# Moving the memory's key and value projection from between the attention steps to between the gathered slots

## What is computed

```python
# first block
h = rms_norm(x); proj = h @ w_in                      # six groups of 512 columns
mq, mk, dq, dk = rope(rms_norm_per_head(...))         # groups 0 to 3; groups 4, 5 are values
x = x + concat(attention_8_heads, differential_attention_4_heads) @ w_out
h = rms_norm(x)
q = h @ peer_query                                    # 8 heads x 2 halves of 128
scores = q . sub_keys                                 # top 16 of each half, top 16 of their 256 sums
# per token and head: 16 experts, so 128 per token
act = gelu(expert_down[e] . h) * gate
x = x + sum_e act * expert_up[e]
# second block
... x = x + mixer(x) @ w_o
k, v = split(rms_norm(mem) @ w_xkv)                   # depends on mem alone
x = x + attention(h @ w_xq, k, v) @ w_xo
x = x + squared_relu_mlp(rms_norm(x)); return rms_norm(x)
```

## Time and profile before

| what | before |
|---|---|
| median of 3 runs | 1484.51 us (1483.87 to 1485.71) |
| the profiled execution's own time | 1484.1 us |
| its span, first to last instruction | 1482.3 us |
| PE, DVE, ACT, POOL busy | 85%, 54%, 41%, 61% |
| bytes moved | 400.70 MB, 268.45 MB of them by the gathers |
| first gather issued, last dot product | 260.0 us, 932.3 us |

### The profile page before, as it was taken

How to read it: one execution, slowest core, us unless ns; L and a number is a source line. 1 busy time by engine, 2 the same in 40 slices (tenths; PEclk the granted TensorE clock), 3 DMA queues, 4 the chain that set the end, 5 groups by cost and what they waited for, 6 DMA issues and landing times.

```text
span 1482.3 us, 17608 instructions
## 1 busy us (share of the span) xinstructions
PE 1264.4 (85%) x5876; PEld 897.6 (61%) x5876; DVE 802.3 (54%) x1512; ACT 600.5 (41%) x1255; POOL 909.5 (61%) x541
## 2 busy tenths in 40 slices
PE   7878888868778877777787787899999989999997
PEld 6667768723333333333333332589999968799886
DVE  5953334287776666677777754251255353259501
ACT  5455544343222333233233222345655435555432
POOL 7973476764444435544444452297878766599985
PEclk9999898979999889889888999899999999999999
DMA  7433345899999999999999999155553744456662
GB/s 250 141 128 107 121 128 179 336 384 420 420 420 420 420 420 420 420 420 421 420 417 418 395 421 406 71 184 186 157 171 117 227 139 144 128 161 196 193 191 99
DMA packets 72944, 400.70 MB, mean 270 GB/s; under 512 B 8096, under 2 KB 8352, under 8 KB 39712
## 3 DMA queue, kind: packets, MB, share of 16 engines
q0 software_dynamic: 36864, 268.45, 43.8%
q1 hardware_dynamic: 33696, 123.35, 26.2%
q10 hardware_dynamic: 2304, 7.85, 1.5%
HBM read 396.48 MB, written 3.15 MB: 270 GB/s over the span
## 4 chain that ended last, share of the span: by engine, by line
PE 29%; issue 22%; POOL 18%; DMA 18%; DVE 11%; ACT 2%; POOLq 0%; ACTq 0%; SPq 0%; DVEq 0%
POOL w_lo L1133 15%; DMA arena<-in_experts,arena 15%; PE bank L689 8%; PE bank L507 6%; PE bank L508 6%; PE bank L509 6%; DMA late_rows<-in_experts,arena 2%; DVE arena L1378 1%; DVE arena L1382 1%; DVE arena L1380 1%; POOL stat L1107 1%; POOL arena L1172 1%; DVE arena L1432 1%; DVE arena L1381 1%; ACT arena L988 1%
## 5 line engine op out<-in xcount | busy, mean ns | idle before, releaser
L1133 POOL TENSOR_TENSOR w_lo<-ring,w_hi 128x1024 fp32r<-128x1024 f32 x228 | 579.1, 2564 | 182.6 <-ACT w_hi L839 182.1
L689 PE MATMUL bank<-arena,diag 128*128 128x512 f32 x872 | 431.6, 653 | 120.4 <-ACT diag L994 120.3
L1172 POOL DMA_INDIRECT arena<-in_experts,arena x218 | 247.5, 1135 | 277.1 <-PE bank L689 225.4
L689 PEld LDWEIGHTS bank<-arena,diag 128*128 128x128 f32 x872 | 180.0, 210 | 369.5 <-issue 226.6
L1432 DVE CUSTOM_DVE_ANT_0 arena<-arena 128x1024 f32<-128x1024 f32 x218 | 262.1, 1225 | 157.7 <-DMA arena<-in_experts,arena 157.5
L839 ACT ACTIVATE w_hi<-ring 128x1024 fp32r<-128x1024 f32 x228 | 240.6, 1059 | 228.0 <-PE bank L509 188.4
L507 PE MATMUL bank<-hT_hi,w_hi 128*128 128x256 f32 x864 | 249.6, 289 | 18.1 <-POOL w_lo L1133 8.2
L508 PE MATMUL bank<-hT_lo,w_hi 128*128 128x256 f32 x864 | 247.3, 286 | 0.0
L509 PE MATMUL bank<-hT_hi,w_lo 128*128 128x256 f32 x864 | 247.1, 286 | 0.0
L985 ACT ACTIVATE arena<-arena 128x4 f32<-128x4 f32 x64 | 13.1, 205 | 439.0 <-DVE arena L1432 439.0
L507 PEld LDWEIGHTS bank<-hT_hi,w_hi 128*128 128x128 f32 x864 | 168.9, 195 | 19.6 <-issue 11.7
(11 more groups left out here) (214 smaller groups left out, 1559.0 us busy)
## 6 DMA issues: line engine op xcount, KB each, us to landing
ring<-in_stream SPq DMA_DIRECT2D x228, 512.0 KB, 3.5
arena<-in_experts,arena POOLq DMA_INDIRECT x218, 18.5
kv_park<-arena ACTq DMA_DIRECT2D x8, 256.0 KB, 3.8
arena<-kv_park ACTq DMA_DIRECT2D x1, 2048.0 KB, 9.1
x_res<-in_x SPq DMA_DIRECT2D x2, 512.0 KB, 5.4
arena<-in_mem SPq DMA_DIRECT2D x1, 1024.0 KB, 11.4
arena<-in_sub_keys ACTq DMA_DIRECT2D x1, 1024.0 KB, 6.3
out<-arena SPq DMA_DIRECT2D x2, 512.0 KB, 2.6
```

The source lines that it names most:

```text
L689: mm = pe.matmul(y_banks[half][:, :], diag[:, slot % DIAGS, :], rows_buf[slot % GATHERS][:, D + 512 * half:D + 512 * half + 512], start=(i ...
L1133: nc.gpsimd.tensor_tensor(w_lo[:, slot, :], ring[:, slot, :], w_hi[:, slot, :].bitcast(F32), ALU.subtract).then_inc(S("lo_made"), 1)
L1172: nc.gpsimd.indirect_dma_start(out=rows_buf[b], out_offset=None, in_=experts, in_offset=bass.IndirectOffsetOnAxis(ap=expert_u[:, slot:slot ...
```

## The change

- The stream's order is `w_in`, `w_out`, `query`, `xk`, `xv`, and the rest as before. PE does `xk` and `xv` ahead of slots 32, 48, 64, 80 (two chunks each), 112 and 152 (four each). ACT copies their results twelve slots later into one of two stages and writes them to DRAM, and makes the high parts there. POOL makes low parts ahead of gathers 60 and 76 (two each), 104, 140 and 184 (four each; the last four are of `in_nat`).
- Eleven buffers up to slot 186, 13 after that, since `hT` must stay until `xv` is done. A second split form `first_hT` serves `w_out` and `query`. `queryT` has two places in place of eight. The dot product writes its elementwise result over the row that it read.
- `sub_keys` and `ffn_rows` are asked for ahead of the norm, with no wait for the writes to DRAM.
- The rotation reads its operand from PSUM, and ACT no longer copies groups 0 to 3. DVE makes the low parts of chunks 3 and 5. The low parts of `w_in` are all made ahead of the memory's norm.
- The last four slots are weighed as 2, 1 and 1.

```diff
+MEMORY_AT = {32: ("xk", 0), 48: ("xk", 1), 64: ("xk", 2), 80: ("xk", 3), 112: ("xv", 0), 152: ("xv", 1)}
+MEMORY_OUT = {slot + 12: piece for slot, piece in MEMORY_AT.items()}
+LOW_AT = {60: 6, 76: 8, 104: 12, 140: 16, 184: 20}
+LAST_BATCHES = [(SLOTS - 4, 2), (SLOTS - 2, 1), (SLOTS - 1, 1)]
+BUFFER = [s % 11 if s < 187 else (s - 176) % GATHERS for s in range(SLOTS)]
-STREAM = [("w_in", 24), ("xk", 8), ("xv", 8), ("w_out", 8), ("query", 16),
+STREAM = [("w_in", 24), ("w_out", 8), ("query", 16), ("xk", 8), ("xv", 8),
...
+DVE_CHUNKS = [FIRST["w_in"] + 3, FIRST["w_in"] + 5]
...
@@ PE, attention steps
             for step in range(16):
-                memory(step)
...
@@ PE, slots
+                    if slot in MEMORY_AT:
+                        memory(*MEMORY_AT[slot])
                     pe.wait_ge(S("diag_made"), slot + 1)
...
@@ ACT, w_in
-                    copy_out(("w_in", n, t), proj1[n][:, t, :])
+                    else:
+                        copy_out(("w_in", n, t), proj1[n][:, t, :])
...
@@ ACT, ahead of the ffn norm
+            act.dma_start(subk, sub_keys).then_inc(S("subk_loaded"), 16)
+            act.dma_start(gain_rows, ffn_rows).then_inc(S("gain_loaded"), 16)
             sumsq("ffn", xs, xn, (0,))
             norm_out("ffn", con("g_ffn"))
             sumsq("ffn", xs, xn, (1,))
-            act.wait_ge(S("kv_parked"), 16 * 8)
-            act.dma_start(subk, sub_keys).then_inc(S("subk_loaded"), 16)
-            act.dma_start(gain_rows, ffn_rows).then_inc(S("gain_loaded"), 16)
...
@@ ACT, slots
+                    if slot in MEMORY_OUT:
+                        name, n = MEMORY_OUT[slot]
+                        park(memory_keys(name, n), name, n)
+                        hi_parts(memory_keys(name, n)[0][1] + RING)
+                    if slot < SLOTS - BATCH:
+                        weigh(slot)
+                    else:
+                        for i, count in LAST_BATCHES:
+                            weigh(i, count)
...
@@ POOL
+                    elif made[0] in DVE_CHUNKS:
+                        pool.wait_ge(S("lo_by_dve"), DVE_CHUNKS.index(made[0]) + 1)
+                        nc.gpsimd.memset(lo_mark[:, i:i + 1], 0.0).then_inc(S("lo_made"), 1)
...
+            lo_parts(LAST["w_in"])
             norm("mem")
-            lo_parts(LAST["xv"])
+            lo_parts(FIRST["w_out"] + RING - 1)
...
+                if slot in LOW_AT:
+                    lo_parts(FIRST["xk"] + LOW_AT[slot] - 1)
...
@@ DVE, rotation
+            low_part(DVE_CHUNKS[0])
...
+            low_part(DVE_CHUNKS[1])
             for g in range(4):
...
-                    qt = pg[:, t * 512:(t + 1) * 512].rearrange("p (h m n) -> p h m n", m=w, n=64)
+                    bank = take(dve, ("w_in", g, t))
+                    qt = bank[:, :].rearrange("p (h m n) -> p h m n", m=w, n=64)
...
@@ DVE, dot
-                if slot >= 2:
-                    dve.wait_ge(S("dots"), slot - 1)
-                v.tensor_tensor_reduce(out=dot_junk[slot % 2], ...
+                v.tensor_tensor_reduce(out=rows_buf[b][:, 0:D], ...
```

More of the change, by code:

```diff
@@ L134, in plan @@
     for step in range(12 + 4):
-        for keys, _, _ in memory_work(step):
-            for key, chunk in keys:
-                add(key, chunk)
         if step < 12:
@@ L144, in plan @@
             add(("pv", step - 4))
-    for keys, _, _ in memory_work(16):
-        for key, chunk in keys:
-            add(key, chunk)
     for g in range(4):
@@ L156, in plan @@
             add(("sub", h - 1))
-    for t in range(TT):
-        for half in range(2):
-            add(("y", t, half))
+    for slot in range(SLOTS):
+        if slot in MEMORY_AT:
+            for key, chunk in memory_keys(*MEMORY_AT[slot]):
+                add(key, chunk)
+        if slot % (SLOTS // TT) == 0:
+            for half in range(2):
+                add(("y", slot // (SLOTS // TT), half))
     norm("mix")
@@ L222, in maps_of, with memory_keys @@
     return [unit] if unit < 8 else [8 + 2 * (unit - 8), 9 + 2 * (unit - 8)]
[L226 to L233 removed]
+def memory_keys(name, n):
+    if name == "xk":
+        return [((name, n), FIRST[name] + 2 * n + 1)]
+    return [((name, n, t), FIRST[name] + 4 * n + 3) for t in range(TT)]
 def split_order():
@@ L315, in build @@
         minus_half = stats(24)
+        lo_mark = stats(2)
         hT = [(hT_hi[:, k, :], hT_lo[:, k, :]) for k in range(KT)]
+        hT_1 = [(first_hT[:, 0, k, :], first_hT[:, 1, k, :]) for k in range(KT)]
+        hT_of = {m: hT_1 if m == "ffn" else hT for m in NORMS}
         xn = tiles(A(0, 2048))
@@ L331, in build @@
         mem, memn = tiles(A(22784, 2048)), tiles(A(24832, 2048))
-        stage = [A(8192 + 512 * i, 512) for i in range(6)] + [A(29440 + 512 * i, 512) for i in range(2)]
+        stage = [A(7168 + 512 * i, 512) for i in range(2)]
         hd_ss = [stats(16) for _ in range(4)]
@@ L628, in _, with memory @@
                 wait_evacuated(pe, ("w_in", 5, t))
-            def memory(step):
-                for _, name, n in memory_work(step):
-                    if name == "xk":
-                        transposed(name, n)
-                    else:
-                        natural(name, 4, n, h_, FIRST[name])
+            def memory(name, n):
+                if name == "xk":
+                    transposed(name, n)
+                else:
+                    natural(name, 4, n, h_, FIRST[name])
             for g in range(4):
@@ L676, in _ @@
                 if h < PEER_H:
-                    transposed("query", h, normed("ffn") if h == 0 else None)
+                    transposed("query", h, normed("ffn") if h == 0 else None, h_1)
                 if h > 0:
@@ L928, in exps, with park @@
                                      accum_out=psums[:, 2 * m + 1:2 * m + 2]).then_inc(S("exps"), 1)
-            def memory_out(step):
-                for keys, name, n in memory_work(step):
-                    for i, (key, _) in enumerate(keys):
-                        piece = n if name == "xk" else 4 + 2 * i + n
-                        copy_out(key, stage[piece])
-                        wait_evacuated(act, key)
-                        act.dma_start(kv_park[:, piece, :], stage[piece]).then_inc(S("kv_parked"), 16)
+            def park(keys, name, n):
+                for i, (key, _) in enumerate(keys):
+                    piece = n if name == "xk" else 4 + 2 * i + n
+                    side = (n if name == "xk" else i) % 2
+                    if parked[side]:
+                        act.wait_ge(S(f"kv_parked{side}"), 16 * parked[side])
+                    copy_out(key, stage[side])
+                    wait_evacuated(act, key)
+                    act.dma_start(kv_park[:, piece, :], stage[side]).then_inc(S(f"kv_parked{side}"), 16)
+                    parked[side] += 1
+            parked = [0, 0]
             act.wait_ge(S("roped"), 4)
@@ L943, in _ @@
                         exps(m)
-                memory_out(step + 2)
                 if step >= 1:
@@ L990, in weigh @@
                 own.sync()
-                for i in range(slot, slot + BATCH):
+                for i in range(slot, slot + count):
                     if i >= DIAGS:
@@ L1007, in _ @@
             sumsq("mix", xs, xn, (1,))
+            for side in range(2):
+                act.wait_ge(S(f"kv_parked{side}"), 16 * 4)
             for a, first, w in c3_parts:
@@ L1278, in _ @@
                  .then_inc(S("head_sums"), 1)
-                for t in range(TT):
-                    wait_evacuated(dve, ("w_in", g, t))
                 pg = proj1[g].rearrange("p t n -> p (t n)")
```

110 lines of the change are left out of this document (61 added, 49 removed).

## The result

The changed kernel takes 1489.74 us (median of 9 runs, 1482.97 to 1496.14) where the kernel before takes 1484.51 (9 runs, 1479.44 to 1487.03): ratio 1.0044, 95% interval 1.0027 to 1.0061. It is 5 us slower. The prediction said 8 us faster. Among all the runs of this document one, of e3, took 1607.8 us in a slower state of the chip; e3's median leaves it out.

The account below looks back on a forecast made before the run. It took the memory path to bound the long gather stage and other waits the stages around it. Ahead of the slots -36, slots +33, end -5: together -8 from 1484.1, so 1476 us, range 1457 to 1492.

Parts of the forecast that it names:

- PE's, ACT's and POOL's part of the 16 chunks among the slots: Slots: memory pieces and low parts mostly fit beside the gathers; +4.5 us, bounds 0 and 14.
- rival 3: Slots: POOL's low parts hold up DVE's dot products, 18.4 us if no queue takes it up; 1494 us, chance 0.11.
- my case with its bounds: Whole kernel: the main forecast, 1476 us, chance 0.50, with its bounds given as 1464 to 1486.
- The buffers' 3.5: Slots: eleven row buffers shorten the gather queue by two slots and slow the first fill; +3.5 us, bounds 0 and +5.
- The bytes' 25.0: Slots: 10.5 MB more of chunks and parked results at 0.420 MB per us, hidden by nothing; +25.0 us.
- Rival 2: Slots: they run dry as PE's memory pieces start at the low clock, about 40 us in place of 4.5; 1511 us, chance 0.10.
- Rival 1: Attention: it gives back its blocks of PE work whole, -36 in place of -18.5 us; 1458.5 us, chance 0.22.
- Rival 4: Input projection: gives nothing since POOL waits for DVE's low parts, rest a few us smaller; 1483 us, chance 0.07.
- The last slots: Last four slots: weighed as 2, 1 and 1, PE has one slot left after the last dot product; -5 us, bounds -3 and -6.
- The attention: Attention: five blocks of PE work leave, DVE's waits shrink, less 3 us for the low clock; -18.5 us, bounds -13 and -36.
- Norm and `sub_keys`: Behind the attention: two products no longer beside low parts, -4 us; PE's wait for `sub_keys` at `query` goes, -6 us.
- The input projection: Start: POOL's lots come 1.3 us earlier each, the wait for chunk 21 goes; -7.5 us, bounds -3 and -11.

Follow-up runs that it names:

- e3: The e1 kernel with POOL's low parts made one at a time, every three to five gathers, instead of in lots of two and four: 1470.6 us.
- e1: The changed kernel with DVE's add of the first tile's results moved four slots ahead, before slot 132 and ahead of the choice of experts: 1477.6 us.
- e6: The kernel before with 11 row buffers instead of 13 from first slot to last, nothing else: 1488.9 us.
- e5: The e1 kernel with each of the eight memory results sent to DRAM twice, 2.1 MB more: 1474.4 us.
- e11: The e1 kernel with only the first of three products of each weight in the six memory pieces on PE: 1472.2 us.
- e2: The changed kernel, add left in place, the two lots of `xv` moved from slots 112 and 152 to 140 and 164: 1477.1 us.
- e13: The kernel before with one line more: POOL makes all low parts of `w_in` before the memory's norm: 1481.3 us.
- e15: The changed kernel itself, unedited, run and profiled a second time: 1488.9 us median, profiled execution 1483.50 us.
- e9: The kernel before with the rotation from PSUM and two chunks' low parts on DVE alone: 1485.0 us.
- e14: The kernel before with both the e9 edit and the e13 line: 1481.6 us.
- e12: The changed kernel with the add still at slot 136 but ahead of the choice of experts instead of behind it: 1476.3 us.

## Why the prediction was wrong

**Where it failed.** The step is "PE's, ACT's and POOL's part of the 16 chunks among the slots", +4.5 with bounds 0 and 14. It asked whether PE has the time for the pieces, and never where their results lie. The pieces move six results in the order in which `plan` gives out eight banks, and the second tile's results thereby move from two free banks into the two of the first tile. That wait was no term, no bound and no rival; the 0.21 for slower stood on other mechanisms. It costs 16.2 us in the slots (e1) and 12.1 in the median. Without it the changed kernel takes 1477.6, where I had forecast 1476. That this is so near is in part luck: in e1's profile the part ahead of the slots gives 32.5 us for 36, the slots cost 29.1 for 33, and the end gives 2.0 for 5. It is luck too that the range holds 1489.7. Its upper edge, 1492, came from rival 3, whose cost did not come; and "my case with its bounds is 1464 to 1486" is narrower than its terms, whose upper bounds, if all come together, sum to 1502.

**Bytes and buffers.** With e1 the slots take 29.1 us more than before, forecast 33. The buffers' 3.5 is what e6 shows. The bytes' 25.0 is not measured as sharply: e5 has 4.1 us for 2.1 MB (5.0 by my price) in one profile, which makes 20 to 25 us of all the bytes and leaves 0.6 to 5 us for the rest of the pieces. e11 puts two thirds of PE's work on them at 1.7 us and e3 the lots of low parts at 0.8, both within the spread: so my 4.5 was probably too high, but that isn't settled. That a piece can outlast the queue shows in e2 behind a choice, not in e1 at slot 112.

**Rival 3's mechanism is there, its cost isn't.** POOL and DVE in the changed kernel:

```profile
515.50 9.22 POOL L1159 TENSOR_TENSOR w_lo<-ring,w_hi 128x1024 fp32r<-128x1024 f32 x4
...
515.88 9.94 DVE L1476 CUSTOM_DVE_ANT_0 arena<-arena 128x1024 f32<-128x1024 f32 x1 [1.20 <-DMA arena<-in_experts,arena]
525.75 1.21 DVE L1476 CUSTOM_DVE_ANT_0 arena<-arena 128x1024 f32<-128x1024 f32 x1
```

One dot product stands for the whole lot, not 2.4 us each of four as I had it; behind it the dots follow at 1.15 us each. The queue covers it (e3: 0.8 us). The rule of the Trainium skill, "SBUF — State Buffer", section "Who interferes with whom", that the later of the two blocks whole, agrees, but in this trace what blocks is the row of four POOL instructions, not one.

**Rival 2** (PE's pieces at the low clock) did not happen: the shares at slots 32 to 80 stay at 1.0, and without two thirds of that work e11's slots gain 1.7 us. **Rival 1** needed -36 in the attention, which gave 26.4 at most. **Rival 4** had POOL wait for DVE's low parts and the start give nothing. POOL does wait for them, 5.4 us in two times, but the first score comes 5.5 to 5.9 us earlier all the same, and the order of POOL's work gave 3 us (e13).

**The last slots**, -5: "the first three slots are done by then" is wrong. It took PE as idle at the last dot product's end, and PE is then in the batch before or just out of it. The step gave 1.1 and 3.4 us in the two profiles.

**The attention**, -18.5: -17.1 in one profile, -26.4 in the other, so my number is the case of the early fall. DVE's waits for values were forecast at 21.6 us. In the changed kernel (waits, 103 to 160 us):

```profile
DVE arena L1385 <- PE bank L635: 18.5, 8, 3.2
DVE arena L1390 <- PE bank L635: 7.7, 4, 2.3
```

and in e15:

```profile
DVE arena L1385 <- PE bank L635: 9.2, 8, 2.3
DVE arena L1390 <- PE bank L635: 7.7, 4, 2.3
```

They are 26.2 us in the first profile and 16.9 in e15. That the clock would have two courses I had not seen, and it makes the changed kernel's runs spread over 13 us (e15's over 20).

**A reading.** The highest slice of the earlier trace rows is 421 GB/s, not the 424 of the text; nothing hangs on it.

**Norm and `sub_keys`**, -4 and -6: -3.2 and -5.9, right, and by the way described (the two products take 1.23 us each, before).

**The input projection**, -7.5: -5.5 to -5.9 in position, but "each lot comes 1.3 us earlier, in three lots 4 us" is wrong, since the add and the scaling, both with two inputs in SBUF, still take 1.96 and 3.29 us beside POOL's lots, and the lots come no closer together. Most of what came is the order's part: it alone gives 4.0 us at the first score (e13), the rotation from PSUM with the two low parts on DVE 2.4 (e9), both together 3.5 (e14), so the two don't add up. The rule of the Trainium skill, "SBUF — State Buffer", section "Who interferes with whom", that a DVE instruction with at most one input in SBUF, outside the two-port modes, does not contend with GpSimd agrees with the 0.41 us; the shorter sum that I drew from it does not.

## What to carry over

When results are moved within an order that hands out buffers in turn, look up for every later result whose buffer it now takes and who frees that when: a move can put a result onto a buffer that is freed late, though no line near it changes. The cure may then be a line elsewhere: free the bank before the long step, not after. Batches at the very end shorten the tail only if the batches before them are short too; and before believing a median of a kernel whose clock has two courses, compare stages of profiles in the same course.

## What the runs showed of the hardware

A lot of four low parts on POOL holds one DVE dot product of 1.22 us for 9.94 us, in e1 for 10.89, and in e12 even a VectorE shift on 128x16 integers for 8.37 us: the hold lasts over the whole row of instructions (9.2 us of POOL's time in each of the three). The same code fell to the lower clock at 105 us in one execution and at 120 us in another, with PE busy 3.39 of the 5 us before 105 us in both (5.00 and 4.16 of the 5 us from 90 us); the first gather came at 227.8 us in the one and at 219.0 in the other.
